# A two-stage ConvFFN with another order of VectorE's, ScalarE's and TensorE's work in its opening and at its stage and round changes

## The reference

```python
def conv_ffn(xn, buf, w_g, w_u, w_c, b_c, w_d):
    g = xn @ w_g
    gc, new_buf = causal_dwconv(g, buf, w_c, b_c)
    return (jax.nn.gelu(gc) * (xn @ w_u)) @ w_d, new_buf
# every layer:  y = y + conv_ffn(rmsnorm(y, g_ffn), ...)   D_MODEL 1024, D_FF 3072, convolution width 3
```

## Time and profile before

| | |
|---|---|
| median of 3 runs | 2572.05 (2571.69 to 2580.36) |
| profiled execution, its own time | 2573.28 |
| span of the profile | 2571.6 |
| mean granted TensorE clock | 0.992 |
| busy share of PE, DVE, ACT, POOL | 96%, 69%, 45%, 37% |

### The profile page before, as it was taken

The page is one execution under the profiler, slowest core; times in us unless marked ns, Lnnn a source line. Parts: engine busy times, 40 slices in busy tenths (PEclk is TensorE's granted clock), DMA queues, the critical chain, the costliest instruction groups (busy, mean ns, idle before and its releaser), DMA issues.

```text
span 2571.6 us, 46180 instructions
## 1 busy us (share of the span) xinstructions
PE 2462.0 (96%) x18693; PEld 2361.4 (92%) x18693; DVE 1769.5 (69%) x2158; ACT 1149.9 (45%) x1851; POOL 959.7 (37%) x623
## 2 busy tenths in 40 slices
PE   7999998899899999998999999998999999989998
PEld 7888786589899999998999999997999999989998
DVE  7466557645877777778778443637878787787775
ACT  5565756533544444443334433525444444443331
POOL 3234333214445453542223411334545454532221
PEclk9999999999899999999999999999999999999999
DMA  5101116852222222336443111122232322265422
GB/s 183 52 27 51 40 29 209 270 192 77 84 102 94 98 102 90 111 125 231 141 141 93 47 49 37 52 75 85 91 116 85 107 93 98 89 235 196 140 89 83
DMA packets 214177, 276.99 MB, mean 108 GB/s; under 512 B 11437, under 2 KB 158998, under 8 KB 210894
## 3 DMA queue, kind: packets, MB, share of 16 engines
q1 hardware_dynamic: 212910, 271.83, 31.7%
q10 hardware_dynamic: 576, 2.10, 0.2%
q0 software_dynamic: 480, 0.11, 0.0%
HBM read 203.57 MB, written 70.43 MB: 107 GB/s over the span
## 4 chain that ended last, share of the span: by engine, by line
PE 64%; DVE 9%; issue 3%; ACT 1%; POOL 1%; DMA 1%; DVEq 0%; ACTq 0%; POOLq 0%
PE psum_all L2159 52%; PE psum_all L2823 7%; PE psum_all L148 3%; DVE down_x_ffn L2110 2%; DVE psum_all L2095 1%; DVE x_residual L2530 1%; DMA w_raw<-in_w_gate_dram 1%; PE psum_all L2875 0%; PE psum_all L2839 0%; POOL rms_scale L1661 0%; DVE x_residual L2481 0%; POOL w_lo_part L113 0%; DVE ffn_x_sums L2418 0%; DVE ffn_x_sums L2404 0%; DVE blocks_down L2099 0%
## 5 line engine op out<-in xcount | busy, mean ns | idle before, releaser
L2159 PE MATMUL psum_all<-ffn_x,blocks 128*128 128x272 f32 x5760 | 736.7, 289 | 24.1 <-DVE ffn_x L2427 13.1
L2159 PEld LDWEIGHTS psum_all<-ffn_x,blocks 128*128 128x128 f32 x5760 | 730.1, 189 | 25.7 <-issue 15.0
L2159 PE MATMUL psum_all<-down_x_ffn,blocks_down 128*128 128x272 f32 x2880 | 375.8, 291 | 25.1 <-DVE x_residual L2530 21.5
L2159 PEld LDWEIGHTS psum_all<-down_x_ffn,blocks_down 128*128 128x128 f32 x2880 | 369.1, 191 | 28.3 <-issue 28.1
L2274 ACT COPY x_residual<-psum_all 128x544 f32<-128x544 f32 x192 | 117.9, 614 | 372.9 <-PE psum_all L2159 369.5
L113 POOL TENSOR_TENSOR w_lo_part<-w_raw,w_hi_part 128x1024 fp32r<-128x1024 f32 x52 | 126.9, 2440 | 355.8 <-ACT w_hi_part L97 355.7
L2530 DVE TENSOR_TENSOR x_residual<-x_residual,psum_all 128x544 f32<-128x544 f32 (+1 forms) x224 | 178.4, 798 | 117.8 <-PE psum_all L2159 116.7
L2481 DVE SCALAR_TENSOR_TENSOR x_residual<-x_residual,ffn_params 128x1088 f32<-128x1088 f32 x96 | 215.0, 2240 | 0.0
L2105 POOL TENSOR_TENSOR x_residual<-x_residual,rms_scale 128x1088 f32<-128x1088 f32 x48 | 152.9, 3185 | 151.8 <-ACT x_residual L2303 151.8
L2466 DVE TENSOR_TENSOR x_residual<-x_residual,psum_all 128x544 f32<-128x544 f32 x144 | 130.3, 905 | 91.4 <-PE psum_all L2159 89.5
L2099 DVE TENSOR_TENSOR blocks<-psum_all,blocks 128x512 fp32r<-128x512 f32 x144 | 99.2, 689 | 122.1 <-ACT blocks L2255 122.1
(11 more groups left out here) (361 smaller groups left out, 4632.6 us busy)
## 6 DMA issues: line engine op xcount, KB each, us to landing
staging_ffn<-hidden_spill SPq DMA_DIRECT2D x54, 816.0 KB, 5.0
hidden_spill<-x_residual SPq DMA_DIRECT2D x24, 1088.0 KB, 4.0
w_raw<-in_w_gate_dram SPq DMA_DIRECT2D x24, 1024.0 KB, 5.4
x_residual<-in_w_up_dram SPq DMA_DIRECT2D x24, 1024.0 KB, 5.2
pages<-in_cache_k_dram SPq DMA_DIRECT2D x64, 256.0 KB, 3.7
pages<-in_cache_v_dram SPq DMA_DIRECT2D x64, 256.0 KB, 4.5
x_spill<-x_residual SPq DMA_DIRECT2D x24, 546.0 KB, 5.5
x_residual<-x_spill SPq DMA_DIRECT2D x24, 546.0 KB, 6.2
```

Source lines behind the costliest of these rows:

```text
L2159: mm = pe.matmul(self.core.ps[:, b + h, 0:HB], wt[:, q * P:(q + 1) * P], xt[:, q, HB * h:HB * (h + 1)], start=first and at == 0, stop=at = ...
```

## The change

What it does, place by place:

- **Opening.** Products of job 0 go in the order B11, T1, B21, B22, T2, NT4, T3 (before: B11, B21, T1, T2, B22, NT4, T3). ScalarE and VectorE have new orders; VectorE makes the low parts of T1 and T3 whole, GpSimd none. TensorE waits for a T's high part ahead of its product and for the low part ahead of the last third. The squares of the last tile are not added by GpSimd; TensorE sums them with matmuls of their own. The last square stands later and in another buffer. The wait for all eight spilled tiles is split in waits for pairs.
- **Stage change.** The scaling of the last pair's gate 0 goes from job 23 to job 24 (behind its sixth block), `down_first` is replaced by `turned_job` and `last_hidden`: sums and low blocks of job 25 stand later, hidden products and sums go between the additions of job 25.
- **Rounds.** `turned_job` and `turn_job` write out VectorE's order in the first and the last job of a round.
- **TensorE in the first job of a round** waits for token highs ahead of a product and for token lows ahead of its last third.

```diff
     def multiply(self, pe, n, i, x_low=None):
         order = [(q, s) for s in range(3) for q in range(depth)]
...
+            if x_low and (q, s) == (0, 2):
+                x_low()
...
                     if m % QUARTERS == 0:
-                        pe.wait_ge(*self.x_lo_done(m // QUARTERS, i))
+                        pe.wait_ge(self.x_hi, 7 * (m // QUARTERS) + i + 1)
...
+                low = None
+                if m >= 0 and m % QUARTERS == 0:
+                    low = lambda: pe.wait_ge(*self.x_lo_done(m // QUARTERS, i))
+                self.multiply(pe, n, i, low)
...
-                if up and (i == 3 or i == 5 and n < JOBS1 - 1):
+                if up and n < JOBS1 - 1 and i in (3, 5):
                     self.gate_scale(pool, t, (i - 3) // 2)
-                elif n == JOBS1 and i == 1:
+                elif n == JOBS1 and i == 5:
+                    self.gate_scale(pool, PAIRS - 1, 0)
                     self.gate_scale(pool, PAIRS - 1, 1)
```

TensorE in the opening, and its sums of squares:

```diff
     def opening(self, pe):
+        def made_first(i):
+            pe.wait_ge(*self.lo_ready(0, i))
+            pe.wait_ge(self.act_lead, self.T_HI[i])
+            self.multiply(pe, 0, i, lambda: pe.wait_ge(self.lead_lo, self.T_LO[i]))
...
         self.multiply(pe, 0, 1)
         pe.wait_ge(self.out.evac, KT)
+        made_first(T1)
+        pe.wait_ge(self.b_lo, 11)
+        pe.wait_ge(*self.lo_ready(0, 0))
+        self.multiply(pe, 0, 0)
+        pe.wait_ge(self.b_lo, 12)
+        pe.wait_ge(*self.lo_ready(0, 4))
+        pe.wait_ge(self.act_out, 1)
+        self.multiply(pe, 0, 4)
+        pe.wait_ge(self.act_out, 2)
+        self.sums_pe(pe, (0, 1))
+        pe.wait_ge(self.dve_out, 1)
+        made_first(T2)
+        pe.wait_ge(self.s_root, 2)
+        made_first(NT4)
+        pe.wait_ge(self.dve_out, 2)
+        self.sums_pe(pe, (2,))
+        pe.wait_ge(self.act_out, 3)
+        made_first(T3)
```

VectorE in the opening (`open_dve` stands between the last two evacuations, `opening_dve` behind the last):

```diff
     def open_dve(self, dve):
         self.block_lo(dve, 0, 2)
+        self.tile_dve(dve, KT - 2)
         self.block_sum(dve, 0, "S4")
         self.block_lo(dve, 0, 3)
         self.block_sum(dve, 0, "S3")
         for q in range(4):
+            self.t1_sum(dve, q)
+        self.t3_sum(dve, 0)
+        self.t3_sum(dve, 1)
+        self.t2_sum(dve, 0)
+        self.block_lo(dve, 0, 4)
+        self.sum_lo(dve, T1)
+
+    def opening_dve(self, dve):
+        self.nt4_sum(dve, 0)
+        self.tile_lo(dve, KT - 1, 0, B21, 0)
+        self.t3_sum(dve, 2)
+        self.t3_sum(dve, 3)
+        self.tile_lo(dve, KT - 1, 1, B22, 1)
+        for q in (1, 2, 3):
             self.t2_sum(dve, q)
+        for q in (1, 2, 3):
+            self.nt4_sum(dve, q)
         self.add_out(dve, 0, 1)
+        self.sum_lo(dve, T2)
+        self.sum_lo(dve, NT4)
         self.block_lo(dve, 0, 6)
+        self.add_out(dve, 0, 4)
+        self.sum_lo(dve, T3)
         self.block_sum(dve, 1, "S1")
         self.block_sum(dve, 1, "S2")
+        self.add_out(dve, 0, 6)
         self.block_lo(dve, 1, 2)
         self.block_sum(dve, 1, "S4")
         self.block_lo(dve, 1, 3)
         self.block_sum(dve, 1, "S3")
-        self.add_out(dve, 0, 6)
```

ScalarE in the opening (old order left out):

```diff
     def opening_act(self, act):
+        for i in range(3):
             self.block_hi(act, 0, i)
+        self.tile_hi(act, KT - 2)
+        self.block_hi(act, 0, 3)
         act.wait_ge(self.out.freed, 1)
         for q in range(4):
+            self.even_copy(act, T1, q, 0)
+        act.wait_ge(self.s_sum, KT - 3)
+        self.block_hi(act, 0, 4)
         act.wait_ge(self.out.freed, 2)
+        self.even_copy(act, T3, 0, 1)
+        self.even_copy(act, T3, 1, 1)
+        self.sum_hi(act, T1)
+        self.even_copy(act, T3, 2, 1)
+        self.even_copy(act, T3, 3, 1)
+        self.square(act, KT - 2)
         act.wait_ge(*self.out.job_done(KT - 1))
         self.block_hi(act, 0, 5)
+        self.tile_hi(act, KT - 1)
         self.block_hi(act, 0, 6)
+        self.square(act, KT - 1)
+        self.copy_out(act, 0, 2)
         self.copy_out(act, 0, 0)
+        self.sum_hi(act, T2)
+        self.sum_hi(act, NT4)
+        self.roots_act(act, (0, 1))
+        self.sum_hi(act, T3)
         self.copy_out(act, 0, 3)
+        self.block_hi(act, 1, 0)
+        self.block_hi(act, 1, 1)
         self.copy_out(act, 0, 5)
+        self.roots_act(act, (2,))
+        for i in range(2, 7):
             self.block_hi(act, 1, i)
```

VectorE at a stage or round change (`last_hidden` is called behind addition i of job 25):

```diff
+    def turned_job(self, dve, n, r):
+        if r == 0:
+            self.piece_lo(dve, 0, T1)
+        self.add_residual(dve, n, 0)
+        if r == 0:
+            self.piece_lo(dve, 0, T2)
+        self.block_lo(dve, n, 6)
+        self.add_residual(dve, n, 1)
+        self.piece_lo(dve, r, B22)
+        self.add_residual(dve, n, 2)
+        self.piece_lo(dve, r, NT4)
+        self.add_residual(dve, n, 3)
+        self.piece_lo(dve, r, T3)
+        self.block_sum(dve, n + 1, "S1")
+        self.add_residual(dve, n, 4)
+        self.block_sum(dve, n + 1, "S2")
+        self.add_residual(dve, n, 5)
+        self.next_lo(dve, n + 1, 2)
+        self.add_residual(dve, n, 6)
+        self.next_lo(dve, n + 1, 3)
...
+    def last_hidden(self, dve, i):
+        t = PAIRS - 1
+        if i < 2:
+            self.hidden_tile(dve, t, i)
+        elif i < 4:
+            for k in ((T1, T3), (T2, NT4))[i - 2]:
+                self.hidden_sum(dve, t, k)
```

More of the change, by code:

```diff
@@ L132, in chunk, with halves @@
     return slice(c * CH, min((c + 1) * CH, USED))
+def halves(tile):
+    return tile.rearrange("p (h n) -> p h n", h=2)
 def width(c):
@@ L2261, in copy_out @@
         r, h, name = {0: (0, 0, "d"), 2: (1, 1, "bb"), 3: (0, 1, "a"), 5: (1, 0, "d")}[i]
-        act.wait_ge(self.product, max(self.done(n, k) for k in range(i + 1)))
+        act.wait_ge(self.product, self.done(n, i))
         if t:
@@ L2282, in tile_act @@
                            ).then_inc(self.b_hi, 1)
-        self.square(act, m)
     def conv_first(self, act, t, r):
```

315 lines of the change are left out of this document (135 added, 180 removed).

## The result

The changed kernel takes 2559.99 (median of 6 runs, 2555.02 to 2563.29), the kernel before 2574.03 (6 runs beside it, 2571.69 to 2580.36): ratio 0.9946, 95% interval 0.9933 to 0.9959, 14 us less. Forecast were 2538, 34 less, and 2517 to 2555 as the range: the time lies above the range. The sign was right; more than half of the gain did not come.

What follows compares the result with a forecast made beforehand. TensorE, busy 96% of the span, was taken to lose its time waiting for VectorE at opening, stage change and round changes. Gains 13 + 13 + 8 = 34 off 2573.28, the median 1.2 lower, gave 2538; range 2517 to 2555.

Steps and rivals of the forecast that it cites:

- Stage change: Change from up to down jobs (jobs 23 to 26): forecast gain 13 over both layers, bounds 4 and 11 each.
- step (e): Job 26: reload of token tiles 4 and 5 comes due, wait 1 to 2; job's fourth product 6.5 earlier per layer.
- (a) to (d): Stage change: moved scaling, later low waits, later sums and low blocks, spread hidden work; job 25's fifth product 8.1 earlier.
- Round changes: Six changes of round: next job due at K+15.75, nearly all idle time gone, gain 13.0, bounds 7 and 13.7.
- Opening: Jobs 0 and 1: one early idle instead of two, new idle of 3.6 in job 1; gain 8 over both layers.
- (a): Stage change: GpSimd's gate 0 scaling leaves the last up job, making all behind it on VectorE 2.3 earlier.
- the rows: Profile rows on the moved scaling: it gives 2.3 where B21 waits and takes back 1.2.
- the rule: Skill's port rule: two-input VectorE and SBUF-reading GpSimd instructions exclude each other, so (a) is worth nothing, stage change 2.3 less per layer.
- New waits absent: Rival: the two new idle times in opening and stage change vanish, 54.7 less, 2518; chance 0.15.
- Slower: Rival: the gate's scale comes late at VectorE's head, 17 us late per layer deciding it, 24 giving 2586; chance 0.03.
- Only the round changes work: Rival: VectorE bounds opening and stage change whatever the order; 11 to 13 us less, 2560; chance 0.07.
- Backlog passed on: Rival: VectorE stays late for a job after each opening and stage change, clock falls twice; 20 less, 2552; chance 0.15.

Runs made afterwards that it cites:

- weights_first: Changed kernel with job 27's raw weights issued ahead of the last hidden store and the reloads; 2548.61, ratio 0.9888.
- rounds_alone: Kernel before with the low waits (round 0 too) and VectorE's new order in rounds 1 to 3, opening and stage-change order as before; 2566.77, ratio 0.9965.
- sums_late: Changed kernel with the next job's sums S1 and S2 behind additions 0 and 1 in each round's second job; 2552.08, ratio 0.9903.
- opening_alone: Kernel before with the new opening alone, all else as before; 2561.18, ratio 0.9947.
- gates_back: Changed kernel with GpSimd's two gate scalings back where the kernel before has them (jobs 23 and 24); 2560.58, ratio 0.9938.
- before_again: Kernel before measured once more, unchanged; 2575.9, ratio 1.0001.
- low_wait_alone: Kernel before with only TensorE's wait for token lows moved to a product's last third, in first jobs of rounds; 2576.57, ratio 1.0003.
- all_four: Changed kernel with job 27's weights early, job 1's first addition early, sums late in rounds' second jobs, TensorE drain ahead of job 2; 2531.39, ratio 0.982.
- add_early: Changed kernel with job 1's first addition ahead of job 2's sums, the second scaling and the tap in the first pair; 2552.69, ratio 0.9907.

## Why the prediction was wrong

**Where the sum failed, in order of size.**

*Stage change, -16.8: step (e) failed.* Both layers (-0.6 and -3.2) lie below the lower bound of 4 each. What (a) to (d) forecast together was about right: job 26 starts 6.7 earlier after the change in layer 0 and 6.9 in layer 1, counted from the start of job 23, where the prediction had 8. Then it loses 7.3 and 10.0 in its fourth product. Step (e) looked for the transfer that comes due and named the token tiles, with a wait of 1 to 2. In weights_first the first addition of job 26 waits 0.52 for them, so they cost little. The one that came due stands behind them in the same queue: job 27's weights, and VectorE's in-order queue puts their sum ahead of the addition that TensorE waits for. The row of SyncE was read the earlier trace rows, but not the row behind it. weights_first shows it: with the weights early, jobs 23 to 26 gain 11.2 over both layers, against 13 forecast. The half-clock stretch behind the wait, which (e) did not have, is about 3 us of it in layer 0: 36 matmuls in 7.52 for 4.5.

*Round changes, -5.6.* With K the start of a round's first job, the next job starts at K+15.8, as forecast. The term that was too small is the 6.5 from the end of addition 5 to the end of the following job's addition 1; from 1252.6 to 1261.2 it was 8.6 in rounds_alone. 1.5 of the missing 2.1 are the two sums at 1.22 and 1.42, beside GpSimd; the rest is an undercount: six low blocks and sums stand there, not four, and addition 6 is a wide one of 1.28. (The recorded sum also does not close: K+15 and 6.5 are K+21.5, not K+21.9; the measured end is K+23.8.) I had weighed the delay by GpSimd in the bound of 7 and did not take it; the measured term, 7.4, lies near that bound. sums_late shows that the two sums' place makes the wait: with them behind the additions it is gone.

*The pace, -5.6.* No term of the sum covered it; below.

*Opening, +5.0.* The mechanism was right in outline: one early wait for two, then a wait for job 1's first addition. Two sizes were off. I took the evacuation at 629.98 as fixed; it stood behind sums on VectorE and moved forward by 4.75, so the wait of 4 that I forecast was 0.27 long. And job 1's wait was 5.36, not 3.6; the two scalings that took 1.7 more than before are nearly all of that. opening_alone measures the term at 15.5, by its ledger 7.6 for each layer, against 4.2 forecast. This error went the other way and hides part of the miss: with the opening as forecast the ledger's 11.8 would be near 6.8.

**(a), the moved scaling.** The prediction chose the rows (worth 2.3 net 1.1) over the rule (worth nothing). gates_back does not decide it: the time is the same within its interval of 0.12% to either side, 3 us, which is more than the 2.2 in question, and jobs 24 and 25 lean to the rows. This stays open; either way it is no large part of the miss.

**Rivals.** *New waits absent* did not come: job 1 and job 25 waited 5.36 and 3.66, longer than forecast. *Slower* did not come: the scaling by the gate's RMS ran at 667.55 without a wait for its roots. *Only the round changes work* gives nearly the measured time, 2560, by luck: it is the opening that works. *Backlog passed on* describes job 26, though the backlog there is one transfer's, not VectorE's own work.

**What stays open.** Jobs 3 to 22 show no idle time and the full clock in all kernels, yet a job takes 21.00 or 21.14. Changed kernel, then opening_alone; two rows of each, one job (168 matmuls) apart:

```profile
796.40 15.26 PE L2196 MATMUL psum_all<-ffn_x,blocks 128*128 128x272 f32 x120
...
817.54 12.75 PE L2196 MATMUL psum_all<-ffn_x,blocks 128*128 128x272 f32 x100
```

```profile
796.67 15.16 PE L2195 MATMUL psum_all<-ffn_x,blocks 128*128 128x272 f32 x120
...
817.67 12.54 PE L2195 MATMUL psum_all<-ffn_x,blocks 128*128 128x272 f32 x99
```

From 796.40 to 817.54 are 21.14, from 796.67 to 817.67 are 21.00. A stretch of jobs keeps its pace from end to end. All ten stretches (two a trace) of before, before_again, low_wait_alone, rounds_alone and opening_alone run at 21.00; of the eighteen stretches of kernels that start from the changed one, nine run at 21.14. Half of those are free of it too, so the two free stretches of opening_alone do not clear the new opening. In stage 2 single rounds show the slower pace, 15.87 a job for 15.77, among them jobs 34 and 35 of layer 1 in low_wait_alone, which has the old opening and the old VectorE orders: the changed code is not needed for it. That all_four has two stretches at 21.14 rules out that a drain cures it. In jobs 3 to 22 it costs an execution 0, 2.8 or 5.6; what sets it was not found.

## What to carry to other kernels

When an order is changed so that a wait ends earlier, list the transfers behind the ones that you moved in each issuing queue, and for each ask which instruction of an in-order engine waits for it and what stands behind that one: here a weight load one place behind a known wait cost 10 us by the medians and 15 in the ledger of jobs 24 to 26. A time of an instruction from the old trace may be carried over as "fixed" only if its own row says that it waited for the engine held fixed. On an engine without gaps, time is won by putting the additions that free PSUM ahead of work for the next job; all_four did this in two places and moved one load, and it tripled the gain (1.8% for 0.5 to 0.7%).

## What the runs showed of the hardware

TensorE's pace at a granted clock of 1.00 has two values, 125.0 and 125.8 ns a matmul of 272 columns on average over a job of 168. The step between starts of matmuls goes through a pattern of four (127, 124, 126, 123 ns in opening_alone) in the first case and of eight (126, 126, 127, 128, 125, 123, 125, 127 ns) in the second.

Half-clock stretches (granted clock 0.50, the 1.2 GHz level) came behind idle times of 3.66, 4.29, 5.36 and 7.72 in the changed kernel; behind the 0.8 to 1.3 of the round changes matmuls ran at full pace. In between, the length of the idle time alone does not tell. Behind 2.08 in job 2 of add_early a product took 3.24 in layer 0 and 4.77 in layer 1; behind 1.99 in job 24 of layer 1 in rounds_alone the next 4 us had a granted clock of 0.59; behind 3.61 in job 25 of layer 1 in sums_late and in all_four it stayed at 1.00. Two round changes of low_wait_alone took 11.50 and 13.02 for the same 90 matmuls, with a granted clock of 1.00 and, in the first 3.8 us, of 0.60:

```profile
1257.57 11.50 PE L2161 MATMUL psum_all<-down_x_ffn,blocks_down 128*128 128x272 f32 x90 [2.04 <-DVE x_residual L2535]
1323.18 13.02 PE L2161 MATMUL psum_all<-down_x_ffn,blocks_down 128*128 128x272 f32 x90 [2.28 <-DVE x_residual L2535]
```

VectorE and GpSimd side by side delayed one another, now one and now the other: three sums of tokens 4.38 beside a GpSimd subtraction of 2.98 in the kernel before, 2.17 beside the same one at 4.40 in rounds_alone.
